# Page copies moved into the column stage, and the memory queries turned behind the value and key projections

## The reference

```
h = rms_norm(x, g);  q_lat, kv_lat, k_rope, conv_in, q_mem, gates = split(h @ w_in)
c = rms_norm(kv_lat);  q = rms_norm_heads(rms_norm(q_lat) @ w_uq);  k = rms_norm_heads([c @ w_uk, k_rope])
y_mla = softmax(rope(q) @ rope(k).T, causal) @ c @ w_uv                  # 8 heads, 128-token blocks
y_mem = softmax(rms_norm_heads(q_mem) @ k_mem.T) @ v_mem                 # 4 heads, 256 memory tokens
# sample tokens: each sequence b attends to 2048 past tokens
c_all  = cache_latent[page_table[b]]   # 16 pages of 128 x 256 float32 each
kr_all = cache_krope[page_table[b]]    # 16 pages of 128 x 32
x = x + (sig(g_a) * y_mla + sig(g_b) * y_conv + sig(g_c) * y_mem) @ w_out
x = x + moe(rms_norm(x))               # 64 experts, top 8, one shared expert
```

## Time and profile before

| what | value |
|---|---|
| median of 3 runs | 2416.02 us |
| profiled execution | 2415.71 us, span 2413.9 us |
| outside the span | 1.8 us |
| busy in the span: PE, DVE, POOL, ACT | 97%, 47%, 32%, 23% |
| column stage | first matmul at 52.0 us, token stage's first at 200.3 us |
| token stage | to the sample stage's first matmul, about 697 us |
| pages copied in the token stage | 128, from 297 to 660 us |

### The profile page before, as it was taken

One profiled execution on the slowest core, in us unless ns is written; L12 is line 12 of the kernel. 1 busy time (PEld: TensorE's weight loads), 2 busy tenths in 40 slices (PEclk: granted clock), 3 DMA queues, 4 the chain that ended last, 5 costly groups with the idle time before them and its releaser, 6 DMA issues. The chain is left out here.

```text
span 2413.9 us, 36532 instructions
## 1 busy us (share of the span) xinstructions
PE 2339.1 (97%) x12668; PEld 1714.0 (71%) x12668; DVE 1141.9 (47%) x2473; ACT 562.3 (23%) x1284; POOL 774.6 (32%) x575
## 2 busy tenths in 40 slices
PE   8999999999999999999999999999999999999995
PEld 5886666666668888766656666568778777877774
DVE  5332545555646656459895256443233333323331
ACT  2001344343523433310013111101111111121211
POOL 1000000000014575500000035435555555666552
PEclk9999999999999999999999999999999999999998
DMA  7521132322238657263113521079999999999996
GB/s 239 165 80 53 30 112 84 93 68 61 65 76 199 167 129 174 75 185 83 40 54 105 186 88 45 18 309 332 332 336 336 348 353 352 359 364 355 357 360 179
DMA packets 286824, 443.53 MB, mean 184 GB/s; under 512 B 122202, under 2 KB 214798, under 8 KB 268122
## 3 DMA queue, kind: packets, MB, share of 16 engines
q1 hardware_dynamic: 250962, 357.25, 44.6%
q0 software_dynamic: 27936, 72.22, 11.9%
q10 hardware_dynamic: 7744, 11.72, 1.3%
HBM read 380.06 MB, written 91.16 MB: 195 GB/s over the span
## 5 line engine op out<-in xcount | busy, mean ns | idle before, releaser
L2720 POOL DMA_INDIRECT mergedT<-tokens_normed,gather_rows x304 | 309.4, 1018 | 121.2 <-issue 95.4
L2834 DVE STREAM_TRANSPOSE xT<-mergedT 128x1280 f32<-128x1280 f32 (+2 forms) x64 | 152.7, 2386 | 282.7 <-DMA mergedT<-tokens_normed,gather_rows 282.6
L2919 PEld LDWEIGHTS pGe<-xT,we_g 128*128 128x128 f32 x2048 | 261.7, 191 | 34.1 <-issue 34.1
L2919 PE MATMUL pGe<-xT,we_g 128*128 128x128 f32 (+4 forms) x2048 | 270.8, 290 | 0.8 <-issue 0.8
L2919 PE MATMUL pUe<-xT,we_u 128*128 128x128 f32 (+4 forms) x2048 | 267.0, 289 | 0.0
L2919 PEld LDWEIGHTS pUe<-xT,we_u 128*128 128x128 f32 x2048 | 260.7, 191 | 0.0
L1661 PE MATMUL pKs<-ws_uk_q,cTs 128*128 128x260 f32 x1024 | 233.6, 384 | 0.0
L2929 PE MATMUL pYe<-we_d,first_w 128*128 128x512 f32 x512 | 230.2, 592 | 0.8 <-DVE first_w L2840 0.8
L1337 POOL TENSOR_TENSOR rk<-ssk,half 128x32 f32<-128x32 f32 x32 | 172.9, 5428 | 130.3 <-DVE ssk L1493 130.3
L1661 PEld LDWEIGHTS pKs<-ws_uk_q,cTs 128*128 128x128 f32 x1024 | 190.6, 190 | 32.8 <-issue 4.3
L2780 ACT ACTIVATE mergedT<-pYe,wc 128x512 f32<-128x512 f32 x128 | 88.1, 688 | 401.9 <-PE pYe L2929 354.2
(11 more groups left out here) (485 smaller groups left out, 3496.0 us busy)
## 6 DMA issues: line engine op xcount, KB each, us to landing
we_g<-in_w_e_gate SPq DMA_DIRECT2D x64, 1024.0 KB
we_u<-in_w_e_up SPq DMA_DIRECT2D x64, 1024.0 KB
we_d<-in_w_e_down SPq DMA_DIRECT2D x64, 1024.0 KB
latents_in_order<-in_cache_latent SPq DMA_DIRECT2D x128, 128.0 KB
lat_quarters<-latents_in_order SPq DMA_DIRECT2D x256, 64.0 KB, 2.2
mergedT<-latents_in_order SPq DMA_DIRECT2D x8, 2048.0 KB, 12.7
first_w<-in_w_in SPq DMA_DIRECT2D x10, 512.0 KB, 5.8
mergedT<-tokens_normed,gather_rows POOLq DMA_INDIRECT x304
```

The costliest lines, as they stand in the source:

```text
L2720: pool.indirect_dma_start(out=xg[v % 2][:, g, :], out_offset=None, in_=quarter, in_offset=bass.IndirectOffsetOnAxis(ap=gi[v % W][:, g:g + ...
L2834: v.transpose(xT[p][:, :, 0:n * GR].rearrange("p c (g i) -> p g c i", g=n), xg[p][:, 0:n, :].rearrange("p g (j c) -> p g c j", c=KD)).then ...
L2919: mm = pe.matmul(dst[p][:, f * CAP:f * CAP + n], w[r][:, k, f * P:(f + 1) * P], xT[p][:, k, 0:n], start=k == 0, stop=k == KD - 1)
```

## The change

Two things move. First, 72 of the 128 pages are copied in the column stage, six in each slot, ahead of the slot's four stores in SP's program; the page table's own load moves there too, and is waited for. The other 56 stay in the token stage, 8 after each unit from unit 3 on. Second, `turn_c` and `take_c` are split: the latents are turned and copied where they were, the memory queries only behind `project_vk`, which now waits for the first copy alone. The filler at `c1` moves with them, and `FILL` gives it in iterations 3 to 7 where it stood in 0 to 4; a half unit each goes from iterations 0, 1 and 2 to 5, 6 and 7. The number of matmuls, DMAs and copies stays.

```diff
@@ ahead of stage_columns
+PAGES_A_SLOT = 6
+EARLY_PAGES = PAGES_A_SLOT * 2 * len(RAW_PAIRS)
+
+
+def line_up(sp, a, keep, i):
+
+    page = sp.value_load(keep.pages[i:i + 1, 0:1], min_val=0, max_val=NPHYS - 1)
+    for dst, name, rows in ((keep.lat_dram, "cache_latent", 16), (keep.kr_dram, "cache_krope", 4)):
+        sp.dma_start(dst[i].rearrange("(r x) c -> r (x c)", r=rows),
+                     a[name][0][bass.ds(page, 1)].rearrange("o (r x) c -> (o r) (x c)", r=rows)).then_inc(keep.paged, 16)
+
+
@@ -151,6 +163,7 @@
                 pair_in(1)
+                sp.dma_start(keep.pages[:, :], a["page_table"].rearrange("b (n o) -> (b n) o", o=1)).then_inc(S["pages_in"], 16)
...
                 sp.dma_start(w_uv[:, :, :], a["w_uv"][0].rearrange("(k p) h n -> p k (h n)", p=P)).then_inc(S["next_in"], 16)
+                sp.wait_ge(S["pages_in"], 16)
                 for s in range(NS):
+                    for i in range(PAGES_A_SLOT * s, PAGES_A_SLOT * s + PAGES_A_SLOT):
+                        line_up(sp, a, keep, i)
                     store(s, 0, "c11_ready", 0, 0)
@@ -489,14 +505,14 @@
 FILL = {
     -1: dict(c0=3, c1=1, s8=2, qk=1, qk1=1),
-    0: dict(c1=1, s7=1, s8=1, qk=1, qk1=1),
...
+    0: dict(s7=1, s8=1, qk=1, qk1=1),
...
-    5: dict(s7=1, s8=1, qk=1, qk1=1),
...
+    5: dict(c1=1, s7=1, s8=1, qk=1, qk1=1),
...
-    7: dict(s1=1, s2=1, s4=1, s5=1, s6=1, s7=1, s7v=1)}
+    7: dict(c1=1, s1=1, s2=1, s4=1, s5=1, s6=1, s7=1, s7v=1)}
 
 
 def stage_tokens(nc, a, o, keep):
@@ -506,7 +522,7 @@
     SLOTS = NHEAD + 2
     GN = TOK // 3
     UNITS = 3 * len(FILL_COLUMNS)
-    FIRST_PAGED = 4
+    FIRST_PAGED = 3
     PAGES = 8
@@ -635,31 +650,22 @@
                 sp.dma_start(causal[:, :], a["k_causal"]).then_inc(S["gains_in"], 16)
                 weights(0)
                 weights(1)
-                sp.dma_start(pages[:, :], a["page_table"].rearrange("b (n o) -> (b n) o", o=1)).then_inc(S["pages_in"], 16)
-
-                def line_up(i):
-                    page = sp.value_load(pages[i:i + 1, 0:1], min_val=0, max_val=NPHYS - 1)
-                    for dst, name, rows in ((keep.lat_dram, "cache_latent", 16), (keep.kr_dram, "cache_krope", 4)):
-                        sp.dma_start(dst[i].rearrange("(r x) c -> r (x c)", r=rows),
-                                     a[name][0][bass.ds(page, 1)].rearrange("o (r x) c -> (o r) (x c)", r=rows)).then_inc(S["paged"], 16)
-
                 for u in range(UNITS):
                     b, g = divmod(u, 3)
                     sp.wait_ge(S["fill_free"], u + 1)
...
-                    if u == FIRST_PAGED:
-                        sp.wait_ge(S["pages_in"], 16)
-                    for i in range(PAGES * (u - FIRST_PAGED), min(PAGES * (u - FIRST_PAGED) + PAGES, DB * NPAGE)) if u >= FIRST_PAGED else ():
-                        line_up(i)
+                    if u >= FIRST_PAGED:
+                        for i in range(EARLY_PAGES + PAGES * (u - FIRST_PAGED), min(EARLY_PAGES + PAGES * (u - FIRST_PAGED) + PAGES, DB * NPAGE)):
+                            line_up(sp, a, keep, i)
...
-                sp.wait_ge(S["paged"], 32 * DB * NPAGE)
+                sp.wait_ge(keep.paged, 32 * DB * NPAGE)
 
@@ -744,12 +750,13 @@
-                def take_c(t):
+                def take_c(t, u):
                     r = rows_of(t)
-                    for u in range(2):
-                        fill_take(t - 1, f"c{u}")
-                        act.wait_ge(S["act_psum"], act_after["c", t] - 1 + u)
-                        act.activation(cT[:, 4 * u:4 * u + 4, 0:r], pA[:, 0:4 * r].rearrange("p (k n) -> p k n", k=4), ACT.Copy).then_inc(S["act_free"], 1)
+                    fill_take(t - 1, f"c{u}")
+                    act.wait_ge(S["act_psum"], act_after["c", t] - 1 + u)
+                    act.activation(cT[:, 4 * u:4 * u + 4, 0:r], pA[:, 0:4 * r].rearrange("p (k n) -> p k n", k=4), ACT.Copy).then_inc(S["act_free"], 1)
+                    if u:
+                        return
                     act.wait_ge(S["c_ready"], t + 1)
...
@@ -828,7 +835,7 @@
                 for t in range(-1, NT):
                     if t >= 0:
                         exps(t, 0)
-                    take_c(t + 1)
+                    take_c(t + 1, 0)
                     if t >= 0:
                         exps(t, 1)
                     for i in range(SLOTS):
@@ -836,6 +843,7 @@
                             exps(t, i + 2)
                         if i == 0:
                             vk_take(t + 1)
+                            take_c(t + 1, 1)
                         if i == 1:
                             q_take(t + 1)
@@ -1044,22 +1052,21 @@
-                def turn_c(t):
+                def turn_c(t, u):
                     r = rows_of(t)
                     pe.wait_ge(S["c_ready"], t + 1)
                     parts = ([cq[0:r, i * P:(i + 1) * P] for i in range(KL)] + [ckv[0:r, i * P:(i + 1) * P] for i in range(KL)],
                              [qmn[0:r, i * P:(i + 1) * P] for i in range(MH)])
-                    for u in range(2):
-                        if u:
-                            fill(t - 1, "c1")
-                        pe.wait_ge(S["act_free"], act_after["c", t] - 2 + u)
-                        for k, src in enumerate(parts[u]):
-                            mm = pe.transpose(pA[:, k * r:(k + 1) * r], src, keep.ident[0:r, 0:r])
-                        mm.then_inc(S["act_psum"], 1)
+                    if u:
+                        fill(t - 1, "c1")
+                    pe.wait_ge(S["act_free"], act_after["c", t] - 2 + u)
+                    for k, src in enumerate(parts[u]):
+                        mm = pe.transpose(pA[:, k * r:(k + 1) * r], src, keep.ident[0:r, 0:r])
+                    mm.then_inc(S["act_psum"], 1)
 
                 def project_vk(t):
                     r = rows_of(t)
-                    pe.wait_ge(S["act_free"], act_after["c", t])
+                    pe.wait_ge(S["act_free"], act_after["c", t] - 1)
                     c_kv = [cT[:, KL + i, 0:r] for i in range(KL)]
                     if t < NT:
                         product("v", t, c_kv, w_uv, 0, NHEAD * VH)
@@ -1086,6 +1093,7 @@
                 def scores(t, i):
                     first = scores_before[t, i]
                     if i == MEM:
+                        pe.wait_ge(S["act_free"], act_after["c", t + 1])
                         for u in range(2):
                             if first + u >= 2:
                                 pe.wait_ge(S["s_free"], first + u - 1)
@@ -1141,7 +1149,7 @@
                     if t >= 0:
                         scores(t, 0)
                     fill(t, "c0")
-                    turn_c(t + 1)
+                    turn_c(t + 1, 0)
                     if t >= 0:
                         scores(t, 1)
                     for i in range(SLOTS):
@@ -1149,6 +1157,7 @@
                             scores(t, i + 2)
                         if i == 0:
                             project_vk(t + 1)
+                            turn_c(t + 1, 1)
                         if i == 1:
                             project_q(t + 1)
@@ -3007,6 +3016,8 @@
                 with Core(nc, keep.spent) as front:
                     keep.mem_v_stored = front.sem("mem_v_stored")
                     keep.raw_stored = front.sem("raw_stored")
+                    keep.paged = front.sem("paged")
+                    keep.pages = front.sb("page_of", [DB * NPAGE, 1], I32)
```

More of the change, by code:

```diff
@@ L114, in stage_columns @@
         S = {n: c.sem("c_" + n) for n in """sums t_sums psum1 psum2 psum3 psum4 psum5 psum6 psum7
-            m1_ready u2_ready u3_ready v5_ready c11_ready c21_ready c22_ready c12_ready next_in""".split()}
+            m1_ready u2_ready u3_ready v5_ready c11_ready c21_ready c22_ready c12_ready next_in pages_in""".split()}
         w_in = [c.sem(f"c_w_in{r}") for r in range(2)]
@@ L491 @@
     -1: dict(c0=3, c1=1, s8=2, qk=1, qk1=1),
-    0: dict(c1=1, s7=1, s8=1, qk=1, qk1=1),
-    1: dict(c1=1, s7=1, s8=1, qk=1, qk1=1),
-    2: dict(c1=1, s7=1, s8=1, qk=1, qk1=1),
+    0: dict(s7=1, s8=1, qk=1, qk1=1),
+    1: dict(s7=1, s8=1, qk=1, qk1=1),
+    2: dict(s7=1, s8=1, qk=1, qk1=1),
     3: dict(c1=1, s7=1, s8=1, qk=1, qk1=1),
     4: dict(c1=1, s7=1, s8=1, qk=1, qk1=1),
-    5: dict(s7=1, s8=1, qk=1, qk1=1),
-    6: dict(s7=1, s8=1, qk=1, qk1=1),
-    7: dict(s1=1, s2=1, s4=1, s5=1, s6=1, s7=1, s7v=1)}
+    5: dict(c1=1, s7=1, s8=1, qk=1, qk1=1),
+    6: dict(c1=1, s7=1, s8=1, qk=1, qk1=1),
+    7: dict(c1=1, s1=1, s2=1, s4=1, s5=1, s6=1, s7=1, s7v=1)}
 def stage_tokens(nc, a, o, keep):
@@ L535, in stage_tokens @@
         causal = c.sb("causal", [P, 4 * P])
-        pages = c.sb("page_of", [DB * NPAGE, 1], I32)
         Sm = [c.sb(f"Sm{r}", [P, SEQ]) for r in range(3)]
@@ L558, in stage_tokens @@
             qk_mean qk_rsq qk_ready act_psum act_free vec_psum vec_free s_psum s_free bias_ready p_ready recip scaled pv_psum o_ready
```

(2 more changed lines are left out.)

## The result

The changed kernel takes 2465.03 us, the median of 4 runs (2461.63 to 2468.60), beside 2416.97 for the kernel before (4 runs). The ratio is 1.0192, 95% interval 1.0165 to 1.0219: slower by about 46 us. Forecast were 2455.6 us with a range of 2443 to 2470, and "slower". The profiled execution took 2461.63 us, 45.9 more than that of before.

The account below looks back on a forecast made before the run. PE was taken to bound the kernel before, SP's queue the changed column stage. 2415.71 + 37.1 (pages) + 2.0 (clock at restart) + 0.8 (queries behind the projection) = 2455.6 us; own range 2447 to 2463, wide range 2443 to 2470.

Parts of the forecast that it names:

- SP bounds the column stage: Column stage: with six pages SP's queue needs 13.7 us a slot, longer than PE's 12.2.
- part 1: Column stage: 72 pages in SP's queue end it at 236.9 us instead of 199.7, +37.1 us.
- PE's late weight pairs lie inside: Column stage: PE loses 3 to 4 us at slots 6, 8 and 10, ending near 209 us, within the 37.
- Half clock at the restart, +2.0: Start of the token stage: after 28 idle us PE runs 4 us at half speed, +2.0 us.
- Part 3: Token stage: memory queries behind the projection, new waits against old waits and half clock gone, +0.8 us (-7 to +9).
- Rival 1: Column stage: SP stays hidden if a page costs under 1.49 us; 2416.5 us, or 2408 with gain; chance 0.06.
- Rivals 2 to 4: SP's queue clogged, 2473 us (0.12); token-stage waits return elsewhere, 2464 (0.08); token-stage edit gains, 2448 (0.08).
- rival 3: Token stage: old waits return elsewhere, +9 instead of +0.8, 2464 us; sign: stage longer by over 5 us; chance 0.08.
- part 2: PE's restart at the token stage: half clock after the idle time, +2.0 us (bounds 0 and 4).

Follow-up runs that it names:

- pages4: The changed kernel with four pages a slot in the column stage instead of six (48 early): 2418.9 us, ratio 1.0003.
- thin_pages: The changed kernel with its 72 early copies cut to 16 elements a row, into scratch, all 128 pages copied whole in the token stage: 2505.9 us.
- bulk_bytes: The changed kernel with each slot's six pages copied into scratch by two large DMAs without register load, all 128 pages copied in the token stage: 2419.4 us.
- turn_only: The kernel before with the changed kernel's `turn_c`, `take_c` and `FILL`, no page moved: 2419.4 us, ratio 1.0005.
- pages_only: The changed kernel with the token stage's old order and old filler table, the 72 pages still in the column stage: 2462.7 us, ratio 1.0194.
- fill_only: The kernel before with the changed kernel's filler table and nothing else: 2411.7 us, ratio 0.9975.
- mix_a: The kernel before with queries turned late in iterations 5 and 6 only, and iteration 7's filler moved from `s1` to `c1`: 2407.6 us, ratio 0.9957.
- pages5: The changed kernel with five pages a slot in the column stage instead of six (60 early): 2441.4 us, ratio 1.0092.

## Why the prediction was right, step by step

- *SP bounds the column stage.* Shown. The step that carried it, a page's queue time taken from the token stage, was right within 2% (2.05 us against 2.01). `pages4`, `thin_pages` and `bulk_bytes` each tell it from traffic. What the page's time consists of was read wrongly: of the gap of 0.8 us ahead of a page, which the prediction put down mostly to the register load, the load is 0.28 us (median of 128, in the kernel before too). So the floor of about 600 ns that it took from the Trainium skill (DMA: Bandwidth & Descriptors, Latency and other measured facts) does not agree with this trace, and half of a page's time is the two issues. The sum does not use it.
- *+37.1 us for part 1* came out as 41.7. Two terms were too small: a store behind pages costs 0.51 us, not 0.36 (2.04 for four), which is 4.3 us in all, and a page 0.045 more, 3.2 us. One was too large: the page table's load held the queue for 1.17 us where it stands now, not 3.23, and the loop began at 64.5 us instead of 67.35, -2.9. The sum of the three, 4.6, is the miss; it is small in part because errors of both signs met.
- *PE's late weight pairs lie inside.* The waits are there (4.5, 2.7 and 5.0 us at slots 6, 8 and 10). PE ended at 216 instead of 209 us, since the prediction had no half clock behind these waits, 5 us of it, and it was still 26 us ahead of the token stage. DVE waited up to 12.6 us for stores, not 7. Neither reached the time.
- *Half clock at the restart, +2.0*: 6 us at 0.50, 2.95 us.
- *Part 3, +0.8*: in `turn_only` the token stage is 2.0 us longer. The new waits are 8.7 us where the sum had 9.2, and 3.0 where it had 2.9; in all, PE is idle for 3.4 us more than before, where the sum had 4.2. The term that was too large is what the clock gives back. No window of `turn_only` from 520 to 680 us is under full clock, as forecast, but PE's busy time in the stage fell by 1.4 us only (481.2 to 479.8), not by 3.4. Each new wait also adds a restart (four value projections take 1.98 us behind a wait, 1.88 without), and no run parts the two. With the clock's 2.95 us this makes 4.95 of the 5.0 us by which the token stage grew.
- That the half clock went with the old waits was in part luck. Iteration 7 has the same wait of 1.67 us in `turn_only`, in the changed kernel and in `bulk_bytes`; in the first two the clock stayed at full speed, in the third it fell. The windows of `bulk_bytes` and then `turn_only`:

```profile
650.00:660.00 10.00, 8.33 (x68) 5.09 (x71) 4.09 (x12) 4.20 (x15) 0.00 (x0) 0.83 0.30 92
```

```profile
650.00:660.00 10.00, 8.34 (x67) 5.18 (x64) 5.04 (x17) 5.26 (x17) 0.00 (x0) 1.00 0.31 89
```

  `pages4` had the fall too. The token stages of `pages4` and `bulk_bytes`, 499.5 and 500.1 us, are 1.2 and 1.7 us longer than that of `turn_only`.
- *Rival 1* (SP hidden) is refuted by `pages_only`; its rule, that the sequencer's time to initiate a DMA "is usually small relative to the DMA itself" (the Trainium skill, DMA: Bandwidth & Descriptors, Issuing engines are not separate DMA queues), is not met here: 2.05 us of queue for 144 KB, while `bulk_bytes` moves the same bytes at no cost. The rival's threshold is right in kind: the kernel is on its other side when a slot has four pages instead of a cheaper page.
- *Rivals 2 to 4* did not occur in the profiled execution: the page average is 2.05, not 2.15. The token stage grew by 5.0 us, which is at the edge of the sign given for rival 3, but 2.95 of it are part 2.
- What the forecast did not look for: that the filler's move was worth 6 us by itself. It priced the change's two token edits as one.

In the profiled execution the forecast was 6.0 us low: 4.6 from part 1, 0.95 from part 2 and 1.2 from part 3, less 0.8 us by which the remainder of the span was shorter. The mechanism held and the sizes were low. The median, 2465.0 us, is 9.4 us above the forecast and 2 us above the forecast's own range of 2447 to 2463; it is inside the wide range only.

Open is the remainder of the medians' 48 us over the traces' 45.9: the profiled execution was the fastest of four that spread over 7 us. In `pages_only` the token stage began at 244.5 us and in the changed kernel at 242.0 with the same program before it: the page loop began 1.4 us later, at 65.8 us, and took 1.1 us more. So SP's queue itself varies by some us, and the clock behind PE's waits varies too, as above; what makes them vary wasn't tried.

## What to carry to other kernels

A queue that computes nothing still has a length. Before work is moved into a stage, multiply the spacing of such issues in the trace by their number and compare it with the stage's own beat, here PE's 12.2 us a slot. Below the beat the work cost nothing (four pages), above it every issue counted (five and six). Copies issued page by page cost queue time for each one, and taking their bytes away did not make them cheaper. Giving them to the queue of another engine was not tried.

When an in-order engine waits for a copy, moving the consumer behind other work can move the wait and not remove it. Here the next user of the same PSUM bank stood directly behind the moved transposes: where there is no filler, a wait of 2.33 us became one of 1.32, and places that had been covered got new ones. Filler put at the wait did better alone than together with the new order (`fill_only` against `turn_only`), and the two chosen place by place did best (`mix_a`).

## What the runs showed of the hardware that was not expected

- A page copy cut to 16 elements a row held SP's queue for 2.63 us, the whole page 1.94 us. Most of the difference is the register load between two copies, 0.75 us instead of 0.28.
- The load of 128 single words (the page table) held the queue for 3.23 us at the head of the token stage (4.40 in `turn_only`) and for 1.17 us at the head of the column stage (1.14 and 1.11 in `pages4` and `pages5`).
- Waits of 1.3 us did not bring the clock down anywhere in the token stage. Waits of 1.67 to 2.36 us did in some traces and not in others, the same wait of 1.67 us among them; a fall behind 1.67 or 1.77 us was 3.4 us long (0.83 on average over 10 us). A wait of 26 us left 6 us at 0.50 behind it, one of 4.2 us an average of 0.74 over the 20 us around it.
